# A second, rounding transfer on the GpSimd queue writes the high halves of the mixers' weight chunks

## The chip, the cores and the metric

The kernel runs on one core of a Trainium2 chip. The metric is device time in microseconds (us). The engines are named as the profile does: PE (TensorE), ACT (ScalarE), DVE (VectorE), POOL (GpSimd) and SP (SyncE, which here only issues transfers).

## The reference

Two blocks in a row work on one sequence of 256 positions and width 1024, all in float32. The first block mixes a gated linear recurrence (a scan) with attention over 64 keys that an indexer picks by top-k, followed by a feed-forward part of width 2816. The second block has two layers; each is a feed-forward part, a mixer and another feed-forward part. Layer 0 mixes a gated product along the sequence with differential attention, layer 1 two kinds of full attention.

```python
def first_block(x, ...):
    h = rms_norm(x, norm_mix_pre[l])
    proj = h @ w_in[l]                       # xr, gr, q, k, v, iq, ik, iw, g_a, g_b
    xc = causal_depthwise_conv(xr, conv_w[l], conv_b[l])
    y_rnn = rg_lru(xc, ...) * jax.nn.gelu(gr)
    y_a = y_rnn @ w_rnn_out[l]
    y_att = dsa_sparse_attention(q, k, v, iq, ik, iw)
    y_b = y_att @ w_att_out[l]
    merged = jax.nn.sigmoid(g_a) * y_a + jax.nn.sigmoid(g_b) * y_b
    x = x + rms_norm(merged @ w_o[l], norm_mix_post[l])
    h = rms_norm(x, norm_ffn_pre[l])
    f = (jax.nn.silu(h @ w_ffn_gate[l]) * (h @ w_ffn_up[l])) @ w_ffn_down[l]
    x = x + rms_norm(f, norm_ffn_post[l])
    return x

def second_block(x, ...):
    for l in range(DEPTH_2):                 # 2 layers
        x = x + 0.5 * swiglu(rmsnorm(x, ffn1_norm[l]), ffn1_w_gu[l], ffn1_w_down[l])
        mix = ...                            # layer 0: gmlp and diff, layer 1: mla and gqa
        x = x + mix
        x = x + 0.5 * swiglu(rmsnorm(x, ffn2_norm[l]), ffn2_w_gu[l], ffn2_w_down[l])
    return x
```

## The kernel before, in words

**Products.** Every matrix product is made of three: high weights by high activations, low weights by high, high weights by low. The high half of a number is its value rounded to the format `float32r` that PE takes at full rate; the low half is what is left. The weights come in 453 chunks of 128 by up to 1024 values (512 KB), in the order in which the products use them. Of these, 123 belong to the mixers (73 in the first, 28 and 22 in the other two), 330 to the feed-forward parts.

**A chunk's way.** `load` (SP's queue) brings chunk i into one of six buffers `RAW`; ACT rounds it into one of six buffers `WH` (line 275); DVE subtracts that from `RAW` and writes `WL` (line 278), after which the load of chunk i+6 is issued. `product` calls `prepare(i + NHL - 1)` ahead of chunk i, so that the rounding and the subtraction of chunk i+4 stand in the engines' queues ahead of what follows chunk i. A slot of `WH` and `WL` is free (`hl_free`) when PE has ended the last product of the chunk six before. `ready` is what PE waits for.

**Order.** The program is written once, in order, into five lists (`Queues`), and each engine works through its own list in order; `op`, `quiet` and `dma` append with the semaphores to wait for. Beside the products runs side work, written as generators (`side`, `pump`): one step of each after every chunk, or every half chunk where a product's output is feature-major. In the first mixer these are `chooser` (indexer, top-k, then attention) and `rnn` (convolution, gates, scan). Before its top-k of each half of the queries, POOL masks the scores (`affine_select`, line 907); DVE then takes eight rounds of `max` and `match_replace` (lines 912 and 913) and two more steps (916 and 917), and POOL masks again (line 918). `later` holds work that is written behind the next product's first block of matmuls. POOL otherwise issues three vectors' or weights' transfers (`GR`, `PGF`, `WS`) at the starts of stages; each waits for all engines (`bar`, `krnn`).

In the first mixer the chunks come in this order: 0 to 4 the indexer's, 5 to 12 `xr`, 13 to 16 keys and values, 17 to 24 queries, 25 to 32 `gr`, 33 to 48 the gates, 49 to 56, 57 to 64 and 65 to 72 the three output products.

Of the kernel before, what the change touches and what calls it, by code (L numbers as in the profile page):

```python
# [11 lines left out]
ACT = mybir.ActivationFunctionType  # L12
# [6 lines left out]
NRAW = 6  # L19
NHL = 6  # L20
# [41 lines left out]
class Queues:  # L62
# [22 lines left out]
    def op(self, eng, fn, *waits):  # L85
        self.count[eng] += 1
        self.q[eng].append((self.flat(waits), fn, eng, 1))
        return (eng, self.count[eng])
# [36 lines left out]
def build(nc, a, out):  # L125
    with ExitStack() as ctx:
        def sb(name, shape, dt=F32, c=ctx):
            return c.enter_context(nc.sbuf_tensor(name, shape, dt))
# [5 lines left out]
        WH = [sb(f"WH{i}", [128, CHUNK], F32R) for i in range(NHL)]  # L134
# [45 lines left out]
        with ExitStack() as c1:  # L180
# [17 lines left out]
        PB = [ctx.enter_context(nc.psum_tensor(f"PB{i}", [128, 512], F32)) for i in range(8)]  # L198

        names = ["pe", "act", "dve", "pool", "sp", "d_x", "d_co", "d_rw", "d_rp", "d_id", "d_bd", "d_ws",  # L200
                 "d_out", "d_x1", "d_pg"] + [f"d_w{i}" for i in range(NRAW)]
        sems = {n: ctx.enter_context(nc.semaphore("s_" + n)) for n in names}

        def col(name, t):
# [7 lines left out]
        def program(plan):  # L212
            Q = Queues()
            op = Q.op
# [43 lines left out]
            hl_free = [None] * NHL  # L258
            ready = {}
            loaded = {}  # L260

            def load(i):
                if i < len(plan):
                    w, k0, kt, c0, n = plan[i]
                    src = a[w][k0 * 128:(k0 + kt) * 128, c0:c0 + n].rearrange("(t p) n -> p t n", p=128)
                    dst = RAW[i % NRAW][:, 0:kt * n].rearrange("p (t n) -> p t n", t=kt)
                    loaded[i] = Q.dma("sp", f"d_w{i % NRAW}", dst, src, raw_free[i % NRAW])

            def prepare(upto):
                while pos["prep"] < min(upto, len(plan)):  # L270
                    i = pos["prep"]
                    pos["prep"] += 1
                    m = plan[i][2] * plan[i][4]
                    raw, hi, lo = RAW[i % NRAW], WH[i % NHL], WL[i % NHL]
                    th = op("act", lambda e, o=hi[:, 0:m], s=raw[:, 0:m]: e.activation(o, s, ACT.Copy),  # L275
                            loaded[i], hl_free[i % NHL])
                    tl = op("dve", lambda e, o=lo[:, 0:m], s=raw[:, 0:m], h=hi[:, 0:m].bitcast(F32):
                            e.tensor_tensor(o, s, h, ALU.subtract), th, loaded[i], hl_free[i % NHL])  # L278
                    raw_free[i % NRAW] = tl
                    ready[i] = (th, tl)  # L280
                    load(i + NRAW)

            def product(w, c0, n, src, tiles, feature_major=False, part=None, carry=None):
# [7 lines left out]
                for k0 in range(lo_k, hi_k, kt):  # L291
# [4 lines left out]
                    if plan:  # L296
                        assert plan[i] == got[-1]
                        prepare(i + NHL - 1)
# [645 lines left out]
            for c in range(2):  # L944
                for f, (bank, tok) in enumerate(product("w_in", c * 512, 512, at0, 8, True)):
                    t = 4 * c + 2 * f
# [14 lines left out]
            for c in range(2):  # L961
                for f, (bank, tok) in enumerate(product("w_in", 1024 + c * 512, 512, at0, 8, True)):
                    t = 4 * c + 2 * f
# [29 lines left out]
            for c in range(2):  # L993
                ks = []
                for b, (bank, tok) in enumerate(product("w_att_out", c * 512, 512, at0, 8)):
                    g, m = GB[:, b, c * 512:c * 512 + 512], GA[:, b, c * 512:c * 512 + 512]
# [255 lines left out]
            return Q, got  # L1252

        _, plan = program([])
        Q, _ = program(plan)

        final = Q.q["sp"].pop()
# [81 lines left out]
```

How the kernel before makes its waits and increments, by code:

```python
    def play(self, eng, e, sems):  # L101
        seen = {}
        for waits, fn, sem, n in self.q[eng]:
            need = {}
            for s, v in waits:
                if v > seen.get(s, 0):
                    need[s] = max(need.get(s, 0), v)
            for s, v in need.items():
                e.wait_ge(sems[s], v)
                seen[s] = v
            ins = fn(e)
            if n:
                ins.then_inc(sems[sem], n)
# [1146 lines left out]
        @block.sync  # L1260
        def _(e):
            Q.play("sp", e, sems)
            for s, v in final[0]:
                e.wait_ge(sems[s], v)
```

## Time and profile before

| | us |
|---|---|
| median of the runs shown (1615.65, 1615.74) | 1615.7 |
| the profiled execution | 1614.28 |
| its span | 1612.7 |
| PE busy | 1462.8 (91%) |
| DVE busy | 931.0 (58%) |
| ACT busy | 757.4 (47%) |
| POOL busy | 9.9 (1%), 18 instructions |
| mean granted TensorE clock | 0.945 |

The page gives averages over stages with different limits; the mixers take about 0 to 375, 762 to 905 and 1282 to 1425 us of the span. An engine's idle time in front of an instruction is put down to what released it. PE's matmuls overlap in the records, so that a matmul that shows 0.39 us follows the one before by 0.23 us.

### The profile page before, as it was taken

The numbers are of one execution on the slowest core, as the hardware profiler recorded it, in microseconds if no ns is written. First come the engines' busy times: TensorE is split into PE (matmuls) and PEld (weight loads), VectorE is DVE, ScalarE is ACT, GpSimd is POOL, SyncE is SP. The second block draws the span as 40 slices with busy tenths as digits, with TensorE's granted clock in tenths as the row PEclk, the third lists the DMA queues.
The fourth block names the chain that finished last, engine by engine and source line by source line (L and its number), as shares of the span: only waits on it lengthen the run. The fifth ranks groups of instructions, "written<-read, shape, count | busy, mean of one in ns | idle before, by whom it ended". The sixth has DMA issues, their size and how long they took to land.

```text
span 1612.7 us, 18442 instructions
## 1 busy us (share of the span) xinstructions
PE 1462.8 (91%) x7100; PEld 1221.6 (76%) x7100; DVE 931.0 (58%) x1474; ACT 757.4 (47%) x1134; POOL 9.9 (1%) x18
## 2 busy tenths in 40 slices
PE   5896678998999999999985999999999974999999
PEld 4885557886888778888764788888888863888887
DVE  4695546566455465555776655545555586565553
ACT  4464575445444354444442544444444453654442
POOL 1000000000000000000000000000000000000000
PEclk9898659998999989999987899999999997999999
DMA  8342104554656545655441456555556540156562
GB/s 252 96 144 78 40 13 169 171 185 142 195 172 195 183 138 181 196 184 187 133 130 40 145 170 201 188 184 183 179 187 196 148 149 1 53 170 195 174 196 75
DMA packets 131766, 242.56 MB, mean 150 GB/s; under 512 B 8544, under 2 KB 21472, under 8 KB 131680
## 3 DMA queue, kind: packets, MB, share of 16 engines
q1 hardware_dynamic: 130480, 238.22, 47.0%
q0 software_dynamic: 624, 2.10, 0.4%
q10 hardware_dynamic: 576, 1.07, 0.3%
q8 instruction: 57, 0.93, 0.2%
q14 instruction: 29, 0.24, 0.0%
HBM read 240.31 MB, written 1.05 MB: 150 GB/s over the span
## 4 chain that ended last, share of the span: by engine, by line
PE 81%; DVE 13%; ACT 4%; issue 1%; DMA 0%; SPq 0%; DVEq 0%; ACTq 0%
PE PB L321 73%; PE PB L349 3%; DVE WL L278 2%; PE PB L482 2%; PE PB L536 1%; DVE T L793 1%; PE PB L523 1%; PE PB L472 1%; DVE SM L402 1%; ACT WH L275 0%; ACT L782 0%; ACT SR L494 0%; DVE SM L387 0%; DVE SM L386 0%; DVE SM L388 0%
## 5 line engine op out<-in xcount | busy, mean ns | idle before, releaser
L278 DVE TENSOR_TENSOR WL<-RAW,WH 128x1024 fp32r<-128x1024 f32 (+1 forms) x453 | 539.2, 1217 | 410.3 <-ACT WH L275 407.2
L275 ACT ACTIVATE WH<-RAW 128x1024 fp32r<-128x1024 f32 (+1 forms) x453 | 466.8, 1053 | 319.2 <-PE PB L321 317.2
L321 PE MATMUL PB<-WH,AT0h 128*128 128x512 f32 (+2 forms) x1328 | 507.8, 382 | 23.7 <-DVE WL L278 15.4
L321 PE MATMUL PB<-WL,AT0h 128*128 128x512 f32 (+2 forms) x1328 | 501.5, 378 | 0.0
L321 PE MATMUL PB<-WH,AT0l 128*128 128x512 f32 (+2 forms) x1328 | 501.3, 377 | 0.0
L321 PEld LDWEIGHTS PB<-WH,AT0h 128*128 128x128 f32 x1328 | 253.9, 191 | 72.3 <-ACT WH L275 11.0
L321 PEld LDWEIGHTS PB<-WH,AT0l 128*128 128x128 f32 x1328 | 253.5, 191 | 45.5
L321 PEld LDWEIGHTS PB<-WL,AT0h 128*128 128x128 f32 x1328 | 253.9, 191 | 43.5
L321 PE MATMUL PB<-WH,FTh 128*128 128x512 f32 x440 | 174.0, 395 | 0.0
L321 PE MATMUL PB<-WH,FTl 128*128 128x512 f32 x440 | 172.5, 392 | 0.0
L321 PE MATMUL PB<-WL,FTh 128*128 128x512 f32 x440 | 170.8, 388 | 0.0
L321 PEld LDWEIGHTS PB<-WH,FTl 128*128 128x128 f32 x440 | 82.6, 188 | 19.3
L321 PEld LDWEIGHTS PB<-WL,FTh 128*128 128x128 f32 x440 | 82.6, 188 | 18.0
L321 PEld LDWEIGHTS PB<-WH,FTh 128*128 128x128 f32 x440 | 82.8, 188 | 16.0
L579 ACT ACTIVATE SR<-PB,SM 128x512 f32<-128x512 f32 (+1 forms) x60 | 39.3, 654 | 98.0 <-PE PB L321 98.0
L587 DVE SCALAR_TENSOR_TENSOR SR<-PB,SM,SR 128x512 f32<-128x512 f32 (+1 forms) x60 | 42.4, 706 | 65.1 <-PE PB L321 65.1
L355 ACT ACTIVATE FTh<-PB 128x512 fp32r<-128x512 f32 x55 | 30.2, 596 | 102.6 <-PE PB L349 102.6
L358 DVE TENSOR_TENSOR FTl<-PB,FTh 128x512 fp32r<-128x512 f32 x55 | 35.7, 687 | 18.1 <-ACT FTh L355 18.1
L321 PE MATMUL PB<-AT0h,WH 128*128 128x256 f32 x128 | 42.8, 334 | 0.0
L523 PE MATMUL PB<-ID,SR 128*128 128x128 f32 x128 | 25.2, 317 | 18.2 <-DVE SR L512 11.3
L321 PE MATMUL PB<-AT0l,WH 128*128 128x256 f32 x128 | 39.9, 312 | 0.0
L321 PE MATMUL PB<-AT0h,WL 128*128 128x256 f32 x128 | 39.7, 310 | 0.0
(279 smaller groups left out, 1191.1 us busy)
## 6 DMA issues: line engine op xcount, KB each, us to landing
RAW<-in_ffn_w_gu_dram SPq DMA_DIRECT2D x88, 512.0 KB, 4.4
RAW<-in_ffn_w_gu_2b_dram SPq DMA_DIRECT2D x88, 512.0 KB, 4.4
RAW<-in_w_in_dram SPq DMA_DIRECT2D x48, 512.0 KB, 4.6
RAW<-in_ffn_w_down_dram SPq DMA_DIRECT2D x44, 512.0 KB, 3.8
RAW<-in_ffn_w_down_2b_dram SPq DMA_DIRECT2D x44, 512.0 KB, 3.6
RAW<-in_w_ffn_gate_dram SPq DMA_DIRECT2D x22, 512.0 KB, 4.4
RAW<-in_w_ffn_up_dram SPq DMA_DIRECT2D x22, 512.0 KB, 4.5
RAW<-in_w_ffn_down_dram SPq DMA_DIRECT2D x22, 512.0 KB, 4.4
```

Source lines behind the costliest of these rows:

```text
L275: th = op("act", lambda e, o=hi[:, 0:m], s=raw[:, 0:m]: e.activation(o, s, ACT.Copy), loaded[i], hl_free[i % NHL])
L278: e.tensor_tensor(o, s, h, ALU.subtract), th, loaded[i], hl_free[i % NHL])
L321: e.matmul(o, l, r, start=s, stop=p, skip_group_check=feature_major)
L349: tok = op("pe", lambda e, o=o, s=src(blk, t): e.transpose(o, s, ID[:, :]), waits, free, ("d_id", 16))
L355: th = op("act", lambda e, o=hi, s=PB[b][:, 0:m]: e.activation(o, s, ACT.Copy), tok, dst.free)
L358: e.tensor_tensor(o, s, h, ALU.subtract), th, dst.free)
L402: k = dve(lambda e: e.tensor_reduce(s3, tmp, AXX, ALU.add), k)
L472: e.transpose(o, s, ID[:, :]), free, kwaits)
L482: e.matmul(o, qt[:, i * 128:i * 128 + 128], r, start=True, stop=True), tq, free, kwaits)
L523: e.transpose(o, s, ID[:, :]), free, tx, krl if lam is not None else None)
L579: tg = [op("act", lambda e, b=b, bank=bank, sl=sl, n=n, rs=rs: e.activation(sl[:, b, :], PB[bank][:, 0:n], ACT.Silu, scale=rs[:, b:b + 1]) ...
L587: k = dve(lambda e, b=b, bank=bank, sl=sl, n=n, rs=rs: e.scalar_tensor_tensor(sl[:, b, :], PB[bank][:, 0:n], rs[:, b:b + 1], sl[:, b, :], ...
```

## The change

From chunk 6 on, the chunks of the mixers (those whose weights' name has no `ffn` in it) get their high half from a transfer on POOL's queue that reads the same weights from HBM again and writes them into `WH` as `float32r`. It waits for `hl_free` alone. The subtraction waits for it in place of ACT. The load into `RAW`, the first six chunks and all feed-forward chunks stay as they are. Six semaphores come on top.

```diff
-                 "d_out", "d_x1", "d_pg"] + [f"d_w{i}" for i in range(NRAW)]
+                 "d_out", "d_x1", "d_pg"] + [f"d_w{i}" for i in range(NRAW)] + [f"d_h{i}" for i in range(NHL)]
...
+            def cast(i):
+                w, k0, kt, c0, n = plan[i]
+                src = a[w][k0 * 128:(k0 + kt) * 128, c0:c0 + n].rearrange("(t p) n -> p t n", p=128)
+                dst = WH[i % NHL][:, 0:kt * n].rearrange("p (t n) -> p t n", t=kt)
+                return Q.dma("pool", f"d_h{i % NHL}", dst, src, hl_free[i % NHL])
+
...
-                    th = op("act", lambda e, o=hi[:, 0:m], s=raw[:, 0:m]: e.activation(o, s, ACT.Copy),
-                            loaded[i], hl_free[i % NHL])
+                    if i >= 6 and "ffn" not in plan[i][0]:
+                        th = cast(i)
+                    else:
+                        th = op("act", lambda e, o=hi[:, 0:m], s=raw[:, 0:m]: e.activation(o, s, ACT.Copy),
+                                loaded[i], hl_free[i % NHL])
```

**POOL, top-k stage of the first mixer, before.** The rows are POOL's instructions in order; `SC` are the scores, `GR` a vector for the end of the mixer.

```order
L907 AFFINE_SELECT SC<-SC 128x128
L918 AFFINE_SELECT SC<-SC 128x128 [waits s_dve]
L907 AFFINE_SELECT SC<-SC 128x256 [waits s_dve]
L918 AFFINE_SELECT SC<-SC 128x256 [waits s_dve]
L95 DMA GR<-in_mix_post_dram 128x1024 [waits s_dve,s_pool,s_act,s_pe]
```

**The same place now** (lines 907 and 918 are 916 and 927):

```order
L95 DMA WH<-in_w_in_dram 128x2x512 [waits s_pe] x9
L916 ISA [waits s_dve]
L916 AFFINE_SELECT SC<-SC 128x128
L95 DMA WH<-in_w_in_dram 128x2x512 [waits s_pe]
L927 AFFINE_SELECT SC<-SC 128x128 [waits s_dve]
L95 DMA WH<-in_w_in_dram 128x2x512 [waits s_pe] x4
L916 AFFINE_SELECT SC<-SC 128x256 [waits s_dve]
L95 DMA WH<-in_w_in_dram 128x2x512 [waits s_pe] x2
L927 AFFINE_SELECT SC<-SC 128x256 [waits s_dve]
L95 DMA WH<-in_w_in_dram 128x2x512 [waits s_pe] x27
```

The transfers of chunks 6 to 14 now stand ahead of the first select, chunk 15 between the first two, 16 to 19 and 20 and 21 between the next, and all later ones behind the last.

**DVE, second half of the top-k stage, now.** `d_h4` and the like are the new semaphores of the slots.

```order
L922 MATCH_REPLACE SC<-SM,SC 128x256 [waits s_dve]
L287 TENSOR_TENSOR WL<-RAW,WH 128x1024 [waits s_pe,s_d_w3,s_d_h3]
L925 TENSOR_SCALAR SC<-SC 128x256 [waits s_dve]
L926 TENSOR_SCALAR SC<-SC 128x256 [waits s_dve]
L287 TENSOR_TENSOR WL<-RAW,WH 128x1024 [waits s_pe,s_d_w4,s_d_h4]
L287 TENSOR_TENSOR WL<-RAW,WH 128x1024 [waits s_pe,s_d_w5,s_d_h5]
L287 TENSOR_TENSOR WL<-RAW,WH 128x1024 [waits s_pe,s_d_w0,s_d_h0]
L287 TENSOR_TENSOR WL<-RAW,WH 128x1024 [waits s_pe,s_d_w1,s_d_h1]
L800 TENSOR_TENSOR T<-T,XC 128x256 [waits s_act]
```

The order on DVE is that of before; only `s_act` has become `s_d_h` in the subtractions' waits. The four subtractions in a row are those of chunks 22 to 25, whose transfers stand behind the last select on POOL.

## Rows read from the trace of the kernel before

**Rows 1.** The page's head and its part 3, DMA queues.

```profile
span 1612.7 us, 18442 instructions
...
q1 hardware_dynamic: 130480, 238.22, 47.0%
q0 software_dynamic: 624, 2.10, 0.4%
```

**Rows 2.** Part 4 of the page, the chain by engine.

```profile
PE 81%; DVE 13%; ACT 4%; issue 1%; DMA 0%; SPq 0%; DVEq 0%; ACTq 0%
```

**Rows 3.** Part 5 of the page, the costliest groups.

```profile
L278 DVE TENSOR_TENSOR WL<-RAW,WH 128x1024 fp32r<-128x1024 f32 (+1 forms) x453 | 539.2, 1217 | 410.3 <-ACT WH L275 407.2
L275 ACT ACTIVATE WH<-RAW 128x1024 fp32r<-128x1024 f32 (+1 forms) x453 | 466.8, 1053 | 319.2 <-PE PB L321 317.2
```

**Rows 4.** Stretches of the span; the first line names the columns.

```profile
core 0: us, PE busy (x) PEld busy (x) DVE busy (x) ACT busy (x) POOL busy (x), PEclk, DMA share, GB/s
92.00:126.00 34.00, 29.27 (x141) 24.62 (x139) 32.56 (x64) 20.55 (x29) 1.61 (x2) 0.99 0.44 132
257.93:314.59 56.66, 56.66 (x242) 46.59 (x243) 29.03 (x26) 27.60 (x31) 0.00 (x0) 0.97 0.69 232
316.50:364.00 47.50, 47.14 (x216) 38.30 (x216) 30.78 (x34) 20.94 (x29) 0.00 (x0) 1.00 0.56 177
262.00:266.00 4.00, 4.00 (x19) 3.27 (x19) 3.26 (x3) 3.10 (x4) 0.00 (x0) 1.00 1.05 387
266.00:270.00 4.00, 4.00 (x19) 3.31 (x18) 1.47 (x2) 1.04 (x2) 0.00 (x0) 1.00 0.99 304
```

**Rows 5.** DVE's longest wait, in 126 to 257 us, then in 755 to 905.

```profile
DVE WL L278 <- ACT WH L275: 33.9, 7, 11.0
...
DVE WL L278 <- ACT WH L275: 19.8, 8, 4.7
```

**Rows 6.** DMA issues: times, KB each, median us to landing.

```profile
GR<-in_mix_post_dram POOLq DMA_DIRECT2D x1, 512.0 KB, 4.2
...
GB<-in_rg_w_a_dram POOLq DMA_DIRECT2D x2, 128.0 KB, 7.5
```

**Rows 7.** Timeline of POOL: start us, us, operation, idle before.

```profile
71.65 0.29 POOL L907 TENSOR_SCALAR_AFFINE_SELECT SC<-SC 128x128 f32<-128x128 f32 x1 [65.67 <-DVE SC L901]
79.37 1.14 POOL L918 TENSOR_SCALAR_AFFINE_SELECT SC<-SC 128x128 f32<-128x128 f32 x1 [7.43 <-DVE SC L917]
...
104.95 1.25 POOL L918 TENSOR_SCALAR_AFFINE_SELECT SC<-SC 128x256 f32<-128x256 f32 x1 [12.59 <-DVE SC L917]
256.70 0.60 POOL L95 DMA_DIRECT2D GR<-in_mix_post_dram  x1 [150.50 <-ACT WH L275]
```

**Rows 8.** Timeline of DVE in the top-k stage.

```profile
74.73 1.22 DVE L278 TENSOR_TENSOR WL<-RAW,WH 128x1024 fp32r<-128x1024 f32 x1
...
79.14 1.22 DVE L278 TENSOR_TENSOR WL<-RAW,WH 128x1024 fp32r<-128x1024 f32 x1
...
104.73 4.83 DVE L278 TENSOR_TENSOR WL<-RAW,WH 128x1024 fp32r<-128x1024 f32 x4
```

**Rows 9.** The chain of waits in time: start us, us, what.

```profile
138.95 1.06 PE PB L482 x4
...
141.74 1.23 DVE WL L278
143.04 0.60 DVE SR L490
```

**Rows 10.** Timeline of DVE, one subtraction in scan, two in mixer two.

```profile
159.35 1.23 DVE L278 TENSOR_TENSOR WL<-RAW,WH 128x1024 fp32r<-128x1024 f32 x1 [4.57 <-ACT WH L275]
...
761.02 1.22 DVE L278 TENSOR_TENSOR WL<-RAW,WH 128x1024 fp32r<-128x1024 f32 x1
...
846.22 1.23 DVE L278 TENSOR_TENSOR WL<-RAW,WH 128x1024 fp32r<-128x1024 f32 x1 [3.69 <-ACT WH L275]
```

**Rows 11.** The chain of waits from 762 us.

```profile
762.62 20.43 PE PB L321 x90
```

## The prediction

> **What bounds the kernel now.** I read the page's head and its chain first, then groups, stretches and waits, then single engines. The span is 1612.7 us [rows 1], and the chain that ended last is PE for 81%, DVE for 13% and ACT for 4% [rows 2]. So most of the time is matrix products, and the feed-forward parts, which the change leaves alone, hold 330 of the 453 chunks. What is left to move lies in the three mixers, where DVE and ACT take the chain. A weight chunk costs ACT 1.05 us for its high half and DVE 1.22 us for its low half [rows 3]. DVE waits for that ACT copy for 407.2 us in all [rows 3], which looks like a prize; but the stretches show that most of it is idle time under a busy PE: from 257.93 to 314.59 PE is busy for all 56.66 us and DVE for 29 [rows 4]. Only where PE is not the bound does that wait cost: 33.9 us of it in the attention and scan stretch of the first mixer, 19.8 us in the second mixer [rows 5]. From 92 to 126 us DVE itself is full, 32.56 of 34 us [rows 4].
>
> **What changes.** 117 of 453 chunks (67, 28 and 22 in the three mixers) lose a 1.05 us ACT copy: 123 us of ACT work. Each gains a second transfer of its bytes and an issue on POOL. The DVE subtraction is still in the same place in its queue, but waits for the transfer.
>
> **Price of a transfer.** Before has no rounding transfer. Plain ones on the same queue took 4.2 us from issue to landing with 512 KB in 4 KB rows, 7.5 us with many small rows in the crowded start [rows 6]; issue took 0.60 us [rows 7]. A chunk has 512 KB in 2 KB rows, so I take the nearest, 4.2, with 7.5 as the upper end, and 0.6 for the issue. Per byte the software queue was no dearer than the hardware one: 2.10 MB for 0.4% of the engines' time against 238.22 MB for 47.0% [rows 1]. An engine that has to round may be slower than any row; that is a rival. By the Trainium skill (DMA: Bandwidth & Descriptors, section "Anatomy of one DMA — SWDGE (gpsimd) path") the fit of 2.0 us plus bytes over 436 GB/s gives 3.2 us for a chunk; no row shows it, GR took 1.0 us more, and with 3.2 the sum would be about 4 us smaller.
>
> A slot comes free when PE ends the chunk six back, and the subtraction of chunk j is queued before the products of chunk j-4. So PE has five chunks of cover (12 products of 0.227 us each [rows 11] make 2.7 us a chunk, so 13.6 us), enough for 4.8 us of transfer and 1.2 of DVE. DVE has only about one chunk of it: if the transfer isn't there, DVE stands still, and all that is queued behind with it.
>
> **Term 1, POOL's queue in the top-k stage: +13.5 us.** POOL is in order and its four selects wait for DVE. Three have transfers behind them that DVE wants at once. (a) The first select ended at 71.94, its follower's subtraction ran at 74.73 [rows 7, 8]: issue and landing give 71.94+0.6+4.2 = 76.7, rounded up for queueing to 77, +2.3. (b) The second select ran 1.14 us to 80.5 [rows 7]; the subtraction behind it ran at 79.14 [rows 8]. It now can't start before 80.5+0.6+4.2 = 85.3, +6.2; less 0.5 us of idle time that DVE had behind it, +5.7. Three more chunks queued there land meanwhile. (c) The fourth select ran from 104.95 for 1.25 us; four subtractions ran from 104.73 [rows 7, 8]. Now 106.2+4.2 = 110.4 at the least with the issue overlapped, +5.7, rounded down to +5.5, since PE's own lag lets the last of the four catch up. All of it counts: DVE is gapless from 92 to 126 and the next stage starts from its rotary step. Ends: 8 (landing 3 us, half absorbed) and 30 (landing 7.5 us, and the four of (c) one after another at two transfers a chunk).
>
> **Term 2, ACT out of the way in attention and scan: -10 us.** At 140.01 PE has the scores; ACT's copy (queued behind its exponentials) lets the subtraction run only at 141.74, and the mask step behind it starts at 143.04 [rows 9]. Its slot had been free for more than a chunk, so the transfer is long there and the mask step can start near 140.3: -2.7. The same happens once more near 149 (-2.7) and at 159.35, after 4.57 us of idle [rows 10], where 2.2 us remain because ACT is needed next anyway. Three further chunks give 0.7, 0.7 and 1.0. Sum -10. Ends: 0, and -17, half of the 33.9 us.
>
> **Term 3, the dense stretch from 258 to 364 us: +4 us.** Before moves 232 GB/s there at a share of 0.69, which is 13.1 MB; 20 more chunks of 0.524 MB make 23.6 MB, or 417 GB/s in 56.66 us. The highest rates with full engines were 387 and 304 GB/s [rows 4], mean 346. At 346 the stretch needs 68.2 us (+11.5), and the next (177 GB/s for 47.5 us, plus 16 chunks) 16.8 MB, 48.6 us (+1). Six slots filled ahead are worth 3.1 MB, 9 us: +3.5, and 0.5 for two product ends at which DVE evicts behind a late subtraction. Ends: 0 (387 GB/s) and +19 (304: 77.7 and 55.3 us, less 10). This is the place where a rule speaks against the change: the Trainium skill (DMA: Bandwidth & Descriptors, "Issuing engines are not separate DMA queues") says that transfers from all queues share the same 16 engines, so a third queue adds no rate. The trace has no pair of full queues to show it; if it failed, this term would be 0.
>
> **Term 4, second and third mixer: +2 us.** On POOL the WS transfer waits for the last residual, which ended as the subtraction at 761.02 [rows 10] began, and that subtraction's own transfer now stands behind WS: about 761.1+0.6+4.2+1.4 (WS's bytes ahead of it at 350 GB/s) = 767.3. From 762.62 PE has 18 products of 0.227 us (20.43 over 90 [rows 11]) before it needs what DVE makes next, until 766.7; DVE now delivers at 767.3+1.2+0.5 = 769.0: +2.3. The first head norm of each mixer starts behind a subtraction whose transfer is just late: +1 each. Against it, the subtraction at 846.22 no longer waits 3.69 us for ACT [rows 10]: -2.5, and the sum is 1.8. Ends: -2.5 and +12.
>
> **Sum.** 13.5 - 10 + 4 + 2 = +9.5 us on the profiled execution's 1614.3, which is 1623.8; the median of the runs shown, 1615.7, stands 1.4 above it, so I predict **1625 us**. A measurement tells 2% (32 us) from no change; this is inside. The rest of ACT's 123 us is costed at nothing: it lies under PE, and nobody waits there.
>
> **Rivals.**
> - *Engines full* (0.17): terms 1 and 3 at their high ends, since loads and transfers queue: 30 + 19 - 6 + 2 = +45, 1660 us. For it: 417 GB/s wanted. Against: the short stretches at 387.
> - *Rounding is slower per byte* (0.15), the case that ends clearly slower: if a rounding byte takes twice an engine's time, 258 to 364 us needs 59.3 MB-equivalents at 346 GB/s, 171 us less 9 of cover against 106: +56; the dense parts of the other mixers, some 24 chunks at 1.5 us, less cover, +25; the selects +14 beyond term 1; 9.5 + 52 + 25 + 14, about +100, 1715 us. It decides once a chunk lands over 11 us after its issue under load, the cover PE has. No row speaks for or against it.
> - *Waits vanish, the queue doesn't block* (0.14): term 1 at 8, term 2 at -17, term 3 at 0, term 4 at -2.5: -11.5, 1604 us.
> - *ACT was the real bound of the mixers* (0.04): both waits of rows 5 go in full, 53.7 us, less term 1 at 13.5: -40, 1575 us. Against it: much of them stands before steps that PE or ACT gate again.
> - If the transfer copies without rounding, low halves become zero, but every instruction runs as long: 1625 too; it is part of the forecast's 0.50.
>
> **Numbers.** Forecast 0.50, spread 1604 to 1648. The range of 1603 to 1680 leaves out the slow rounding and the last rival, just under 2 in 10. Faster by over 2%: 0.04. Slower by over 2% (from 1648): the slow rounding 0.15 and most of the full-engines case 0.12, together 0.27. Within: 0.69.
>
> **What would show it.** ACT's busy time near 635 us; POOL with 117 more issues. Term 1: DVE waits for a transfer of 2 to 6 us before the subtractions behind the selects, and reaches its rotary step near 140 instead of 126 us. Term 2: no wait for ACT before subtractions up to the end of the scan, and that stretch about 10 us shorter. Term 3: DMA share near 1 and over 330 GB/s between 270 and 370, PE gaps small. Feed-forward parts unchanged to 1 us. I am wrong in size if landing takes over 7 us alone, and wrong in kind if the top-k stage isn't longer.

## The result and the profile after

The changed kernel takes 1647.45 us in the median of two runs (1644.56 and 1650.35), against 1615.7 us before. The ratio is 1.0197 with a 95% interval of 1.012 to 1.0274: slower beyond the noise, since the interval leaves out 1, but whether by more or less than 2% two runs can't say. The profiled execution took 1644.56 us, its span is 1642.9 us. The forecast was 1625 in a range of 1603 to 1680; the direction and the range held, and the loss is three times the 9.5 us of the sum.

In the changed kernel a line behind the new function stands 9 lines lower than before: the subtraction is L287, the ScalarE copy L284, the products L330.

The head of the page, its queues, the chain by engine and the two groups that answer to [rows 3]:

```profile
span 1642.9 us, 18413 instructions
...
q1 hardware_dynamic: 130480, 238.22, 45.5%
q0 software_dynamic: 32704, 62.27, 13.2%
...
PE 77%; DVE 13%; ACT 4%; DMA 4%; issue 2%; POOL 0%; SPq 0%; DVEq 0%; POOLq 0%
...
L287 DVE TENSOR_TENSOR WL<-RAW,WH 128x1024 fp32r<-128x1024 f32 (+1 forms) x453 | 540.3, 1216 | 425.1 <-ACT WH L284 292.8
...
L284 ACT ACTIVATE WH<-RAW 128x1024 fp32r<-128x1024 f32 x336 | 347.7, 1058 | 263.1 <-PE PB L330 263.1
```

The 117 copies are gone (453 to 336, 119 us of ACT). DMA, which had 0% of the chain [rows 2], now has 4%, some 66 us in which the chain runs through a transfer. Per byte the rounding transfers were a tenth dearer, far from twice: 62.27 MB took 13.2% of the engines' time (0.212% a MB), the plain loads 0.191% a MB. That closes the rival of slow rounding.

Where the time went is read best as a shift: the start of the same PE instruction in both traces, after minus before, at the ends of the prediction's stages. The other columns are experiments told below, each from its own profiled execution. In after it grows only inside stages that a term names. e4, e8 and e12 carry a step of 7 to 10 us behind 1350.96 that the last section tells of; the profiled execution was the slowest one of each of these three.

| PE at (us in before) | stage that ends there | after | e1 | e2 | e3 | e4 | e8 | e12 |
|---|---|---|---|---|---|---|---|---|
| 129.84 | top-k | +11.2 | +12.9 | +0.6 | -0.1 | -0.9 | +7.4 | -0.7 |
| 257.93 | attention, scan | +9.1 | +11.9 | -5.9 | 0.0 | -1.4 | +7.5 | +0.2 |
| 369.35 | dense stretch | +23.2 | +13.0 | -6.1 | +13.3 | -1.6 | +5.6 | -1.6 |
| 730.47 | feed-forward | +21.6 | +11.2 | -6.0 | +13.5 | -1.8 | +3.9 | -1.6 |
| 822.89 | mixer two, projections | +30.8 | +11.0 | -5.9 | +13.6 | +8.3 | +8.8 | +1.6 |
| 900.80 | mixer two, attention | +26.6 | +8.6 | -5.9 | +13.6 | +8.5 | +6.2 | +2.6 |
| 1350.96 | mixer three, projections | +30.3 | +9.0 | -5.9 | +13.6 | +16.3 | +8.3 | +6.2 |
| span's end | | +30.2 | +9.8 | -5.9 | +13.6 | +26.1 | +17.8 | +12.8 |

So after has +11.2 (term 1: forecast +13.5), -2.1 (term 2: -10), +14.1 (term 3: +4), then -1.6 in the feed-forward part, +5.0 in mixer two and +3.7 in mixer three (term 4: +2 for both).

**Term 1.** POOL's timeline in the top-k stage answers to [rows 7], DVE's to [rows 8]:

```profile
71.50 0.29 POOL L916 TENSOR_SCALAR_AFFINE_SELECT SC<-SC 128x128 f32<-128x128 f32 x1 [10.17 <-DVE SC L910]
71.92 0.72 POOL L95 DMA_DIRECT2D WH<-in_w_in_dram  x1
80.49 0.28 POOL L927 TENSOR_SCALAR_AFFINE_SELECT SC<-SC 128x128 f32<-128x128 f32 x1 [7.85 <-DVE SC L926]
80.92 2.88 POOL L95 DMA_DIRECT2D WH<-in_w_in_dram  x4
...
110.08 0.39 POOL L927 TENSOR_SCALAR_AFFINE_SELECT SC<-SC 128x256 f32<-128x256 f32 x1 [11.12 <-DVE SC L926]
110.52 4.31 POOL L95 DMA_DIRECT2D WH<-in_w_in_dram  x6
```

```profile
75.84 1.23 DVE L287 TENSOR_TENSOR WL<-RAW,WH 128x1024 fp32r<-128x1024 f32 x1 [1.18 <-DMA WH<-in_w_in_dram]
...
85.01 1.23 DVE L287 TENSOR_TENSOR WL<-RAW,WH 128x1024 fp32r<-128x1024 f32 x1 [4.68 <-DMA WH<-in_w_in_dram]
...
115.36 5.28 DVE L287 TENSOR_TENSOR WL<-RAW,WH 128x1024 fp32r<-128x1024 f32 x4 [5.43 <-DMA WH<-in_w_in_dram]
...
137.10 0.22 DVE L423 TENSOR_TENSOR T1a<-QKI,RP 128x64 f32<-128x64 f32 x1
```

Right behind each select stand the transfers that had piled up: one, four, then six in 4.31 us. DVE waits 1.18, 4.68 and 5.43 us before the subtractions behind them, and its rotary step starts at 137.10 instead of 125.84.

**Term 3.** Stretches of after that answer to [rows 4], and the transfers' landing (KB each, median us):

```profile
core 0: us, PE busy (x) PEld busy (x) DVE busy (x) ACT busy (x) POOL busy (x), PEclk, DMA share, GB/s
267.05:323.94 56.89, 56.89 (x241) 46.67 (x242) 26.34 (x23) 4.78 (x9) 14.12 (x20) 0.96 1.08 352
323.94:387.12 63.18, 52.56 (x225) 42.68 (x223) 34.84 (x39) 10.65 (x18) 7.86 (x11) 0.92 0.85 271
```

```profile
WH<-in_w_in_dram POOLq DMA_DIRECT2D x43, 512.0 KB, 4.8
...
WH<-in_w_rnn_out_dram POOLq DMA_DIRECT2D x8, 512.0 KB, 8.1
WH<-in_w_att_out_dram POOLq DMA_DIRECT2D x8, 512.0 KB, 8.2
```

The engines are full: 352 GB/s at a share of 1.08 (the times of all packets are added up, so a share can pass 1), and its stretches of 10 us from 272 to 322 moved 329 to 383 GB/s, where the loads alone had reached 387 [rows 4]. The Trainium skill (DMA: Bandwidth & Descriptors, "Issuing engines are not separate DMA queues") says that transfers of all issuing engines run on the same 16 DMA engines; the trace agrees. But in that very stretch PE loses nothing: 56.89 of 56.89 us. The loss is in the next one, behind 323.94 us, where one product ends and the next begins. I call this place the seam. DVE's and PE's timelines there show why:

```profile
324.87 1.23 DVE L287 TENSOR_TENSOR WL<-RAW,WH 128x1024 fp32r<-128x1024 f32 x1 [2.38 <-PE PB L358]
327.56 1.23 DVE L287 TENSOR_TENSOR WL<-RAW,WH 128x1024 fp32r<-128x1024 f32 x1 [1.47 <-DMA WH<-in_w_att_out_dram]
328.70 1.28 DVE L994 TENSOR_TENSOR XR<-XR,PB 128x512 f32<-128x512 f32 x2
329.90 1.28 DVE L367 TENSOR_TENSOR AT0l<-PB,AT0h 128x512 fp32r<-128x512 f32 x2
```

```profile
330.68 0.76 PE L330 MATMUL PB<-WH,AT0h 128*128 128x512 f32 x1 [5.71 <-DVE AT0l L367]
331.25 0.63 PE L330 MATMUL PB<-WL,AT0h 128*128 128x512 f32 x1
331.67 0.63 PE L330 MATMUL PB<-WH,AT0l 128*128 128x512 f32 x1
```

PE's transposes had begun at 323.94. Their eviction AT0l, with which the next product starts, stands in DVE's queue behind two subtractions that are late. Both waited for their transfer: the row puts the first wait down to PE's transposes, but that chunk's transfer, issued at 316.16, landed only at 324.84. PE stands 5.71 us. At the same place before it stood 1.07:

```profile
316.53 0.47 PE L321 MATMUL PB<-WH,AT0h 128*128 128x512 f32 x1 [1.07 <-DVE AT0l L358]
```

Then products follow each other every 0.42 us instead of 0.227: the clock is at its lower level there, and 0.78 granted in the mean of 324 to 334 us. Two more product ends with a PE wait for DVE (1.56 and 3.35 us) follow in the same way. Of the 14 us that the stretch loses, the three waits make 9.6 (the 1.07 of before taken off) and slow products the rest.

### The profile page after: what moved, and what is told of

Read it like the earlier page. It is cut to its first block, busy times and chain, and to the rows that moved or that the text cites. A ratio compares the mean times of both kernels' runs of the same rounds, so it can differ in the third digit from the quotient of the medians.

```text
span 1642.9 us, 18413 instructions
## 1 busy us (share of the span) xinstructions
PE 1472.3 (90%) x7100; PEld 1226.8 (75%) x7100; DVE 930.9 (57%) x1474; ACT 644.3 (39%) x1017; POOL 91.4 (6%) x135
## 3 DMA queue, kind: packets, MB, share of 16 engines
q0 software_dynamic: 32704, 62.27, 13.2%
q10 hardware_dynamic: 576, 1.07, 0.2%
HBM read 300.47 MB, written 1.05 MB: 184 GB/s over the span
## 4 chain that ended last, share of the span: by engine, by line
PE 77%; DVE 13%; ACT 4%; DMA 4%; issue 2%; POOL 0%; SPq 0%; DVEq 0%; POOLq 0%
PE PB L330 69%; PE PB L358 3%; DVE WL L287 2%; PE PB L491 2%; PE PB L545 2%; DMA WH<-in_ev_w_in_dram 1%; DVE T L802 1%; PE PB L532 1%; DMA WH<-in_w_att_out_dram 1%; DMA WH<-in_w_in_dram 1%; PE PB L481 1%; DVE XC L776 1%; DVE SM L411 0%; ACT L791 0%; DVE SM L396 0%
## 5 line engine op out<-in xcount | busy, mean ns | idle before, releaser
L287 DVE TENSOR_TENSOR WL<-RAW,WH 128x1024 fp32r<-128x1024 f32 (+1 forms) x453 | 540.3, 1216 | 425.1 <-ACT WH L284 292.8
L330 PE MATMUL PB<-WH,AT0h 128*128 128x512 f32 (+2 forms) x1328 | 510.0, 384 | 38.9 <-DVE WL L287 21.5
L330 PE MATMUL PB<-WL,AT0h 128*128 128x512 f32 (+2 forms) x1328 | 502.8, 379 | 0.0
L330 PE MATMUL PB<-WH,AT0l 128*128 128x512 f32 (+2 forms) x1328 | 502.3, 378 | 0.0
L284 ACT ACTIVATE WH<-RAW 128x1024 fp32r<-128x1024 f32 x336 | 347.7, 1058 | 263.1 <-PE PB L330 263.1
L330 PEld LDWEIGHTS PB<-WH,AT0h 128*128 128x128 f32 x1328 | 254.6, 192 | 89.7 <-issue 38.9
L330 PEld LDWEIGHTS PB<-WH,AT0l 128*128 128x128 f32 x1328 | 254.3, 191 | 46.0
L330 PEld LDWEIGHTS PB<-WL,AT0h 128*128 128x128 f32 x1328 | 255.0, 192 | 43.4
L330 PE MATMUL PB<-WH,FTh 128*128 128x512 f32 x440 | 174.0, 395 | 0.0
L330 PE MATMUL PB<-WH,FTl 128*128 128x512 f32 x440 | 172.5, 392 | 0.0
L330 PE MATMUL PB<-WL,FTh 128*128 128x512 f32 x440 | 170.8, 388 | 0.0
L330 PEld LDWEIGHTS PB<-WH,FTl 128*128 128x128 f32 x440 | 82.6, 188 | 19.3
L330 PEld LDWEIGHTS PB<-WL,FTh 128*128 128x128 f32 x440 | 82.6, 188 | 18.0
L330 PEld LDWEIGHTS PB<-WH,FTh 128*128 128x128 f32 x440 | 82.8, 188 | 16.0
L364 ACT ACTIVATE FTh<-PB 128x512 fp32r<-128x512 f32 x55 | 30.2, 596 | 102.9 <-PE PB L358 102.9
L330 PE MATMUL PB<-AT0h,WH 128*128 128x256 f32 x128 | 43.2, 338 | 0.0
L568 ACT ACTIVATE JK<-X 128x512 bf16<-128x512 f32 x28 | 17.4, 623 | 63.5 <-DVE X L621 47.3
L95 POOL DMA_DIRECT2D WH<-in_w_in_dram x43 | 30.7, 717 | 206.4 <-PE PB L330 184.4
L330 PE MATMUL PB<-AT0l,WH 128*128 128x256 f32 x128 | 40.3, 315 | 0.0
```

The lines of the kernel that those rows point to most:

```text
L95: self.q[eng].append((self.flat(waits), lambda e: e.dma_start(dst, src), sem, 16))
L330: e.matmul(o, l, r, start=s, stop=p, skip_group_check=feature_major)
L364: th = op("act", lambda e, o=hi, s=PB[b][:, 0:m]: e.activation(o, s, ACT.Copy), tok, dst.free)
L568: ts.append(op("act", lambda e, blk=blk, ss=ss: e.activation(JK[:, blk, :], X[:, blk, c * 512:c * 512 + 512], ACT.Square, accum_out=ss[:, ...
```

## The experiments

Unless said otherwise each is the changed kernel with another choice of chunks. Medians are compared with the runs of before on the same chip: 1614.52 us for e1 to e8, 1614.07 for e9 to e12. A single run of before lay between 1609.9 and 1620.7, so only differences of some 3 us between medians mean anything.

**e1 to e4: the change in four parts.**

```diff
-                    if i >= 6 and "ffn" not in plan[i][0]:
+                    if 6 <= i < 31:                                  # e1
+                    if 31 <= i < 43:                                 # e2
+                    if 43 <= i < 73:                                 # e3
+                    if i >= 205 and "ffn" not in plan[i][0]:         # e4
```

> Transfers for chunks 6 to 30 alone (up to the rotary step), ScalarE copies elsewhere. Theory (the selects on POOL's queue hold up the transfers behind them, and nothing later takes it back): +11 us on the kernel before, 1627 (1624 to 1630), DVE's rotary step at 137 us as in the changed kernel. Rival (the loss of the top-k stage is absorbed by waits of the attention stage): the rotary step at 137, but the end within 4 us of before.

Measured 1625.44 us, ratio 1.0071 (1.0052 to 1.0091): +10.9. The theory holds, with DVE's rotary step at 138.70 us in place of 137. In the profile PE is 12.9 us late at the end of the stage and 9.8 at the end of the span, so later stages took back little.

> Transfers for chunks 31 to 42 alone, those that are prepared in the attention and scan stretch. Theory (DVE's waits for the ACT copy only turn into waits for PE, which has the same products between the scores): -2 us, 1614 (1611 to 1616). Rival (the forecast's term of -10 was right, and the late entry into the stretch or its transfers hid it): 1606 (1603 to 1609).

Measured 1608.39 us, ratio 0.9963 (0.9949 to 0.9978): -6.1, faster. Outside the theory's range and inside the rival's, though 4 us short of the forecast's -10. I take up below what after lost of it.

> Transfers for chunks 43 to 72 alone, the dense rest of the first mixer. Theory (the +14 us between 267 and 392 us are made there, by subtractions that wait for their transfer and the steps queued behind them on DVE): +13 us, 1629 (1625 to 1632). Rival (it was made by the late state that the earlier transfers left): under +6, below 1622.

Measured 1627.63 us, ratio 1.008 (1.0065 to 1.0095): +13.1. The theory holds. PE's longest wait is at the same seam, with nothing changed ahead of it:

```profile
PE PB L330 <- DVE AT0l L367: 6.2, 1, 6.2
```

> Transfers in the second and third mixer alone. Theory (the shift from 21.8 to 30.2 us after 740 us is made there and independent of the first mixer): +8 us, 1624 (1620 to 1627). Rival (part of the offset is only the run's own spread): below +4.

Measured 1627.38 us (1623.02 to 1640.35), ratio 1.0093 (1.0059 to 1.0127): +12.9, above the theory's range. The four parts add up to 10.9 - 6.1 + 13.1 + 12.9 = +30.8 us, and the whole change costs +31.75. So the medians need no large interaction. That the sums agree to 1 us is in part chance: the whole is the median of two runs, e4's interval reaches from 9.5 to 20.5 us, and by the table attention and scan gave 6.5 us in e2 and 2.1 in after.

**e5, e6: the selects.** e6 is the kernel before without POOL's four selects, which leaves out the causal mask of the scores; e5 is e1 without them.

```diff
-                    k = op("pool", lambda e, blk=blk, nk=nk, wk=wk: e.affine_select(
-                        out=wk, in_=SC[:, blk, 0:nk], compare_op=ALU.is_ge, fill=MASKED, base=128 * blk,
-                        pattern=[[-1, nk]], channel_multiplier=1), kacc, bar)
+                    wk, k = SC[:, blk, 0:nk], (kacc, bar)
...
-                    k = dve(lambda e, wk=wk: e.tensor_scalar(wk, wk, -BIG, None, ALU.add), k)
-                    k = op("pool", lambda e, blk=blk, nk=nk, wk=wk, bi=bi: e.affine_select(
-                        out=bi, in_=wk, compare_op=ALU.is_ge, fill=-BIG, base=128 * blk,
-                        pattern=[[-1, nk]], channel_multiplier=1), k, bar)
+                    k = dve(lambda e, wk=wk, bi=bi: e.tensor_scalar(bi, wk, -BIG, None, ALU.add), k, bar)
```

> As the kernel with transfers for chunks 6 to 30 alone, but without POOL's four selects (the causal mask of the index scores is left out; DVE's steps are as many and as large). Theory (a select that waits for DVE holds the transfers behind it): the +10.9 us go, it ends within 2 us of the kernel before without the selects, about 1614 (1610 to 1617). Rival (the transfers' own landing time costs it): at least +8 stay, 1622 or more.

> The kernel before without the four selects, the base for the last one. Both theories: within 3 us of before, 1612 (1609 to 1616), since DVE has other work while POOL selects.

Measured 1613.12 us for e5, ratio 1.0003 (0.9985 to 1.0022), and 1613.63 for e6, ratio 0.9993 (0.9976 to 1.0009). The transfers are all there (25 of 512 KB, landing 5.1 us), and the +10.9 us are gone. What the top-k stage lost was POOL's order, not the price of transfers. DVE's timeline of e5 ahead of its rotary step:

```profile
123.01 3.49 DVE L287 TENSOR_TENSOR WL<-RAW,WH 128x1024 fp32r<-128x1024 f32 x3
126.42 0.22 DVE L423 TENSOR_TENSOR T1a<-QKI,RP 128x64 f32<-128x64 f32 x1
```

**e7: half the bytes.** e3, with each transfer cut to the first half of its chunk.

```diff
                 w, k0, kt, c0, n = plan[i]
+                kt = kt // 2
```

> As the kernel with transfers for chunks 43 to 72 alone, but each moves only the first half of its chunk (the other half of the high tile keeps old values). Theory (full DMA engines make the landing late, 8 us where it is 5 elsewhere, and DVE's evictions stand behind it): landing near 4.5 us, and of +13.1 at most +4 stay, 1616 (1613 to 1619). Rival (any landing after the slot is free, 4 us where ACT took 1, is late enough for the product ends): +9 or more, 1624 or above.

Measured 1616.65 us, ratio 1.0021 (1.0000 to 1.0042): +2.1 of +13.1 stay. Landing in e3 first, then in e7:

```profile
WH<-in_w_rnn_out_dram POOLq DMA_DIRECT2D x8, 512.0 KB, 8.4
WH<-in_w_att_out_dram POOLq DMA_DIRECT2D x8, 512.0 KB, 9.1
```

```profile
WH<-in_w_rnn_out_dram POOLq DMA_DIRECT2D x8, 256.0 KB, 5.1
WH<-in_w_att_out_dram POOLq DMA_DIRECT2D x8, 256.0 KB, 4.0
```

DVE's waits barely shrink before the seam (12.7 us for the first of these weights, 13.4 in e3). What shrinks is what PE feels: it stands 2.58 us at the seam in place of 6.2, 2.5 in place of 4.5 at the two product ends behind it, and the products run at the higher level of the clock.

```profile
316.93 0.47 PE L331 MATMUL PB<-WH,AT0h 128*128 128x512 f32 x1 [2.58 <-DVE AT0l L368]
317.24 0.39 PE L331 MATMUL PB<-WL,AT0h 128*128 128x512 f32 x1
```

So the loss goes with the landing, which is 8 to 9 us while the engines are full and late enough for one eviction. This run alone can't part it from the rate, since half the bytes change both; e8 can.

**e8: the subtraction later.** All transfers of the changed kernel, but DVE's subtraction is put into its queue two chunks behind the transfer.

```diff
+LAG = 2
...
+                while pos["cast"] < upto:
+                    i = pos["cast"]
+                    pos["cast"] += 1
+                    if i >= 6 and "ffn" not in plan[i][0]:
+                        high[i] = cast(i)
                 while pos["prep"] < upto:
                     i = pos["prep"]
+                    if i in high and i >= upto - LAG:
+                        break
...
-                    if i >= 6 and "ffn" not in plan[i][0]:
-                        th = cast(i)
+                    if i in high:
+                        th = high[i]
```

> The changed kernel, but DVE's subtraction of a chunk is queued two chunks later than its transfer is issued. Theory (the loss is DVE standing at the head of its queue for a transfer, with evictions, selects' inputs and norms behind it): most of terms 1, 3 and 4 goes and the gain of term 2 stays, 1612 (1606 to 1620); DVE's waits for transfers fall from 115 us to under 40. Rival (the transfers' rate itself is short, so PE waits instead): 1635 or more, with PE waiting for the low halves.

Measured 1623.13 us (1618.55 to 1632.12), ratio 1.0062 (1.004 to 1.0085): +8.6 where the change had +31.75. Neither side came out whole. DVE's waits for transfers fell from 126.8 us (the sum of its eight rows in after) to 70.1, not below 40. By the table the top-k stage keeps +7.4 and the mixers' later stages still cost, but the shift is +5.6 both at 263.66 (in before) and at 369.35: the dense stretch costs nothing, where it cost +14.1. Yet every transfer is there and the engines are as full as in after. PE is busy throughout, and at the seam it stands 1.0 us, as before the change. The stretch, then PE's wait at the seam:

```profile
263.00:320.00 57.00, 57.00 (x252) 47.01 (x251) 24.58 (x22) 4.79 (x8) 15.55 (x22) 1.00 1.12 370
...
PE PB L340 <- DVE AT0l L377: 1.0, 1, 1.0
```

That leaves the rival of a short rate no place in the dense stretch: what costs there is the subtraction that stands for its transfer ahead of an eviction. Attention and scan give only 1.8 us here. Behind the scan PE now waits 8.8 us for a subtraction, against 5.1 at 257.93 in before. Most of the whole loss (23 of 31.75 us) hangs on when DVE comes to stand before a transfer; e1's part of it is POOL's order, which a later subtraction only softens.

**e9: neither copy nor transfer.** e2 with the work itself left out; the low half, formed as raw minus the old high tile, takes up the difference.

```diff
-                        th = cast(i)
+                        th = hl_free[i % NHL]
```

> Chunks 31 to 42 get their high half neither by a copy nor by a transfer (the tile keeps old values, so that part of the weights is left out). Theory (in the attention and scan stretch a transfer is as good as no work at all, since its slot is free early): as with transfers for these chunks alone, 1608 (1606 to 1611). Rival (transfers still cost there, by landing or by a selected start): 1603 or less.

Measured 1606.9 us, ratio 0.9958 (0.9941 to 0.9975): -7.2. e2's transfers had given -6.1. So 7 us is all that this stretch gives when these twelve chunks need neither a copy nor a transfer, and the forecast's 10 was not there to be had.

**e10: the lag without a transfer.** The kernel before; each ScalarE copy stays where it was, DVE's subtraction is queued one chunk later.

```diff
+LAG = 1
...
+                while pos["copy"] < upto:
+                    i = pos["copy"]
+                    pos["copy"] += 1
+                    m = plan[i][2] * plan[i][4]
+                    high[i] = op("act", lambda e, o=WH[i % NHL][:, 0:m], s=RAW[i % NRAW][:, 0:m]:
+                                 e.activation(o, s, ACT.Copy), loaded[i], hl_free[i % NHL])
-                while pos["prep"] < min(upto, len(plan)):
+                while pos["prep"] < upto - LAG or (upto == len(plan) and pos["prep"] < upto):
...
+                    th = high[i]
```

> No transfer at all: the kernel before, with the ScalarE copy of every chunk as early as before and DVE's subtraction of it queued one chunk later. Theory (the gain in attention and scan comes from DVE no longer standing behind a late copy): -5 us, 1609 (1606 to 1613), and DVE's 407 us of waits for ACT fall below 100. Rival (the gain comes from ACT's own queue being shorter by 1.05 us a chunk, which this does not change): within 2 us of before.

Measured 1614.97 us, ratio 1.0011 (0.9999 to 1.0022): no change. My theory fell on the time, and on the waits: DVE still waits 240.7 us for ACT (407.2 before). In its profiled execution DVE has no wait for a copy left in attention and scan, and PE gains 3.5 us there up to 219 us of before; 2.1 of them are gone again by 264. Part of e2's gain may so come from DVE's place in the queue and the rest from ScalarE's shorter queue, but the run doesn't show it: the medians are the same, and between e5, e6 and before, with the same work in this stretch, the profiles differ by 1 us there as well.

**e11: a second place.** e2, and transfers for the output projection that mixer two prepares during its attention (`or 225 <= i < 233`).

> Transfers for chunks 31 to 42 and for 225 to 232, the output projection that is prepared in the second mixer's attention. Theory (both are stretches in which slots are free early and PE is not full): 6.1 less for the first, 2 more for the second, 1606.5 (1604 to 1609). Rival (the second group stands where PE or a product end waits for it): 1610 or more.

Measured 1607.96 us, ratio 0.9975 (0.996 to 0.999); e2 had 1608.39. The 2 us more aren't there. Its profiled execution is 2.5 us shorter between 823 and 901, but e1, which has no transfer there, is 2.4 shorter as well.

**e12: the WS transfer off POOL.** e4 with one transfer moved to ScalarE's queue.

```diff
-                kws = Q.dma("pool", "d_ws", WS[:, :, :], a["ws"], bar)
+                kws = Q.dma("act", "d_ws", WS[:, :, :], a["ws"], bar)
```

> As the kernel with transfers in the second and third mixer alone, but the WS transfer is issued by ScalarE's queue. Theory (DVE's wait of 7.5 us behind WS is one of two large waits of the second mixer; the other, behind the residual, stays): 3 us less than with WS on POOL, 1624 (1619 to 1628); no wait of DVE for a transfer over 5.5 us between 785 and 800. Rival (WS costs nothing, the product ends cost all): 1627 or more, and PE at the rotary step of the second mixer as late as before this edit (+8 us).

Measured 1624.18 us, ratio 1.0067 (1.0048 to 1.0085): 3.2 less than e4 in the medians, as the theory had it, but the two intervals overlap, so the size isn't shown. The place is: in the profiled executions mixer two up to its rotary step costs +3.2 instead of +10.1 us, and DVE's only wait for a transfer between 785 and 800 us is this one:

```profile
DVE WL L287 <- DMA WH<-in_ev_w_in_dram: 1.5, 1, 1.5
```

POOL's timeline of after shows what the transfers had stood behind, and DVE's what came of it:

```profile
787.04 0.56 POOL L95 DMA_DIRECT2D WS<-in_ws_dram  x1 [9.50 <-PE PB L358]
787.59 1.43 POOL L95 DMA_DIRECT2D WH<-in_ev_w_in_dram  x2
```

```profile
784.01 1.23 DVE L287 TENSOR_TENSOR WL<-RAW,WH 128x1024 fp32r<-128x1024 f32 x1 [4.33 <-DMA WH<-in_ev_w_in_dram]
785.15 1.28 DVE L621 SCALAR_TENSOR_TENSOR X<-PB,X 128x512 f32<-128x512 f32 x2
...
793.91 1.23 DVE L287 TENSOR_TENSOR WL<-RAW,WH 128x1024 fp32r<-128x1024 f32 x1 [7.48 <-DMA WH<-in_ev_w_in_dram]
795.05 1.65 DVE L378 SCALAR_TENSOR_TENSOR AT0l<-PB,CO,AT0h 128x256 fp32r<-128x256 f32 x4
```

**The version that beats both** is e2: transfers only for the twelve chunks prepared in the first mixer's attention and scan, 1608.39 us, 0.4% below before (0.2 to 0.5 by its interval) and 2.4% below the change.

## Why the prediction was right in kind and too small

**The number.** The range held, but it was 77 us wide, and the sum was 21 us short of the profile's +30.2: 10 us in term 3, 8 in term 2 and 7 in term 4, less 2 in term 1 and 1.6 in the feed-forward part. So each place was named rightly and three of four terms were mis-sized, term 3 most.

**What bounds it.** Right. Products are the chain, DVE's position decides the rest, and the feed-forward parts moved by -1.6 us over 361 us. That is more than the 1 us I named, but e1 and e6 show -1.8 and -1.6 there with nothing changed in that part.

**Price of a transfer, 4.2 us: right alone, wrong under load.** Issue 0.72 instead of 0.6 us, landing 4.8 us in the median of the first 43, but 8.1 and 8.2 in the dense stretch. The upper end of 7.5 was a row of a crowded start [rows 6], and I used it only for term 1. Taken for term 3 it would have made each subtraction at a product end some 3 us later. The estimate from the Trainium skill (DMA: Bandwidth & Descriptors, "Anatomy of one DMA — SWDGE (gpsimd) path"), 3.2 us, was lower than every 512 KB median of after.

**Term 1, +13.5: right.** Measured +11.2. (a) The first follower ran at 75.84, 3.9 us after its issue where 4.8 had been reckoned, so +1.1 and not +2.3. (b) The second ran at 85.01, which is near the 85.3 by luck: that figure left out the delay of (a), and without it (b) is +4.8 and not +5.7. (c) The four began at 115.36, 10.6 us late; the fourth select itself was 5.1 us late, and 5.5 came on top, as forecast. e5 shows that the selects are the cause.

**Term 2, -10: the direction was right, the size failed.** I gave a wait nearly its full length in each case ("the mask step can start near 140.3: -2.7"). The waits for ACT did go, all 33.9 us of them [rows 5]. But PE has products between the scores in its order, and what DVE no longer waited for ACT it waited for PE. DVE's wait for PE in 126 to 258 us of before, then in 137 to 267 us of after:

```profile
DVE QKI L540 <- PE PB L536: 16.1, 6, 9.6
```

```profile
DVE QKI L549 <- PE PB L545: 40.6, 10, 9.6
```

The limit is 7.2 us (e9), the transfers reach 6.1 of it (e2), and after shows 2.1. Most of what is left between e2 and after lies in the clock. Stretches of e2, then of after, at about the same place in the program:

```profile
173.00:181.00 8.00, 7.78 (x56) 6.79 (x56) 4.77 (x11) 5.21 (x18) 0.72 (x1) 0.94 0.26 64
```

```profile
185.00:193.00 8.00, 8.00 (x35) 6.79 (x35) 2.95 (x9) 3.36 (x13) 0.71 (x1) 0.50 0.05 5
```

And the same place before:

```profile
175.00:183.00 8.00, 8.00 (x36) 6.89 (x35) 3.61 (x9) 4.18 (x14) 0.00 (x0) 0.50 0.24 67
```

In 8 us PE does 56 instructions at 0.94 and 35 at 0.50. Up to 161 us (in the time of before) the changed kernel had gained 2.0 us and e2 2.7; behind that the changed kernel ran at the lower level, as the kernel before had done, and e2 did not. So 3 of e2's 6 us are made where its clock is at the higher level while that of before is not, and a sum of waits had no place for them. What decides which level it is, the runs don't show.

**Term 3, +4: the term that was mis-sized most.** It was built as 3.5 us of missing rate plus 0.5 for "two product ends at which DVE evicts behind a late subtraction". The measured parts are the other way round: no loss in the stretch whose rate I had priced (PE 56.89 of 56.89 us), then some 14 us at three product ends and in the slow clock behind them. The mechanism was named and priced at 0.5 us. Its first wait alone is 5.71 us against 1.07, and my sign "PE gaps small" failed with it. e3 shows that the place is right, e7 that the loss goes with the landing, and e8 that it is gone, at 370 GB/s, once the subtraction stands later in DVE's queue.

**Term 4, +2: too small.** WS was forecast at +2.3, on the reasoning that PE has 18 products of cover. Behind the subtraction at 793.91, though, stands the norm's low half AT0l, which PE needed after those 18. And the last residual itself was 3.7 us later than PE's shift of 21.6, behind the subtraction at 784.01. e12 puts WS's share of e4 at 7 us in the profiles and 3 in the medians, the latter within the noise. The head norms that I put at +1 each stand behind more than one late chunk: mixer three adds +3.7 in after and +7.8 in e4. The -2.5 at 846.22 can't be told apart: after is 4.2 us shorter from 823 to 901, but e1 is 2.4 shorter and has no transfer there.

**The rivals.** Full engines (0.17, 1660 us) was the nearer one: the measured median, 1647.45, lies between it and the forecast, at the edge of the forecast's own spread of 1604 to 1648. The rival's mechanism (PE starved by a short rate) isn't what happened in the dense stretch (e8). Slow rounding, vanishing waits and ACT as the real bound are ruled out by the queues' rows, by e1 and by e9.

## What to carry to other kernels

Work moved to a transfer saves the engine but lengthens the time from a free slot to a ready tile, here from a copy of 1.05 us to a landing of 4.8 us, and of 8 to 9 under load. Price that at every place where a step that PE needs next is queued behind the consumer, and add the slow products behind PE's pause (there were some after 5.71 us, none after 2.58). A queue that issues transfers must not hold a step that waits for compute; and a wait that vanishes is worth only what the next engine in the loop can give, which a run with the work left out measures in one go.

## What the runs showed of the hardware

**After one long pause the clock came back some 3 us later in one trace and some 25 us later in another.** Behind DVE's rotary work in mixer three PE stands for about 20 us. Before, the clock is back within the second of these stretches; in e11, which changes nothing after 905 us, it isn't in two:

```profile
1344.00:1354.00 10.00, 3.04 (x15) 2.90 (x16) 7.37 (x16) 1.39 (x3) 0.00 (x0) 0.50 0.00 0
1354.00:1364.00 10.00, 9.19 (x48) 6.18 (x46) 2.69 (x9) 7.47 (x23) 0.00 (x0) 1.00 0.01 2
```

```profile
1344.00:1354.00 10.00, 9.92 (x28) 5.95 (x27) 0.86 (x2) 5.18 (x12) 0.00 (x0) 0.50 0.01 2
1354.00:1364.00 10.00, 10.00 (x30) 6.64 (x29) 2.71 (x8) 4.73 (x17) 0.00 (x0) 0.50 0.00 0
```

PE did 28 and 30 instructions in 10 us where it did 48. In before it starts again at 1350.96 and the clock is at its higher level from 1354; in e11 it starts at 1341.01, is shown busy nearly all the time, and the clock stays at its lower level until about 1366. e11's lead of 10.0 us at 1350.96 of before was 0.5 us at 1366.56. e4 and e8 lose 9.4 us at the same place, and e4's five runs spread over 17 us. e11's ten runs fit this: seven lie at 1605.6 to 1609.3 us and three, the profiled one among them, at 1613.0 to 1614.1. A profile of one execution can carry such a step, so a small difference has to be read stage by stage or from ten runs.

**POOL's second and fourth select took 1.14 and 1.25 us before [rows 7], and 0.28 and 0.39 in after**, with the same shapes. The Trainium skill (Perfetto Trace Analysis, "GPSIMD Engine Instruction") says to treat the span of a GpSimd instruction as unreliable; these rows are a case of it or of a real difference, which no run here tells apart.
